# Routing weights of the first 128 tokens added into a DRAM table by GpSimd's indirect DMAs, those of the second 128 by one-hot products

## The chip, the cores and the metric

The kernel runs on one core of one Trainium2 chip. The metric is the device time of one execution in microseconds (us). The engines are TensorE (PE, with its weight loads PEld), VectorE (DVE), ScalarE (ACT), GpSimd (POOL) and SyncE (SP, which here issues DMAs only). ACT and POOL issue DMAs too.

## What is computed

Two transformer-like layers on 256 tokens of width 1024, in fp32. The change touches only the expert lookup ("peer") of the first layer. Of the reference, cut to that part:

```
qry = rms_norm((hb @ w_query).reshape(128, 8, 256), query_gain)      # hb: a block of 128 tokens
s1 = einsum("thd,nd->thn", qry[..., :128], sub_keys_1)                # (token, head, 128 keys)
s2 = einsum("thd,nd->thn", qry[..., 128:], sub_keys_2)
v1, i1 = top_k(s1, 16);  v2, i2 = top_k(s2, 16)
cand_s = v1[..., :, None] + v2[..., None, :]                          # 16 x 16 sums for each token and head
cand_i = i1[..., :, None] * 128 + i2[..., None, :]
top_s, pos = top_k(cand_s, 16)
experts = take_along_axis(cand_i, pos);  gates = softmax(top_s)
act = gelu(einsum("thkd,td->thk", expert_down[experts], hb))
out = einsum("thk,thkd->td", gates * act, expert_up[experts])
```

There are 128 x 128 = 16384 experts, and each token picks 8 x 16 = 128 of them.

## The kernel before, in words

The kernel gathers no expert rows. It computes gelu(hb @ expert_down) for all 16384 experts and all 256 tokens, multiplies it by a table G of gates that is zero where an expert was not picked, and multiplies the product by expert_up. Each fp32 factor of these large products is split into a high and a low float32r part: ACT writes the high part of a weight unit (128 x 512 words) in `split_hi` (L285), DVE the low part in `split_lo` (L290), and PE then does three products for each pair of tiles. There are four buffers of split units: ACT waits until PE is done with the unit four before (`unit_used`), DVE waits for ACT, PE waits for DVE. The weights themselves come by 1 MB DMAs from SP into a ring of four slots (`Stream`), four units each.

The stage in question is the Block at L1791. Its first part, "down", has 256 units (u = 0 to 255), 12 matmuls each (L1833). Every 8 units ACT applies Gelu to one group of 4 x 256 results (`gelu`, L1876) and stores it in `act_spill`. Everything else is woven between the units, in the order in which the code is written:

- DVE: `routing()` is a generator. After each unit's `split_lo`, DVE takes two or three of its steps (L2030): top 16 of 128 scores for 32 rows, sums, top 16 of 256 for 16 rows, then, for each tile of 128 tokens, the two key numbers of each pick by comparing with an iota, multiplying and reducing 128 x 2048 words. It must be finished at u = 154 (L2032). `step` (class `Steps`) attaches a semaphore to an instruction and makes DVE wait for it.
- ACT computes Exp of all picks at u = 155 (L1908), DVE divides by the sums, PE transposes the picks (L376) and DVE copies them out (L2043).
- From u = 161 to 247, six units of each eight carry a batch of gates of four tokens (`slots`, L1765). For a token DVE builds two one-hot matrices (L2007, L2010, `gated_onehots`), PE multiplies them (L1819), and the product is the token's 128 x 128 slab of gates; ACT copies four slabs from PSUM into G (L1897). There are 64 batches.

The second part, "up" (256 units, L300), loads the stored activations back in 32 pieces (`load_acts`, L1886), multiplies them by G (`weights`, L2017), splits them and multiplies by expert_up. POOL has nothing to do from the Block's start until `store_gate` and `load_gate` near its end. G lies on the words O_R and up; the routing's own scratch lies there as well, above its 83rd of 128 expert rows (`CLEAR`).

## Time and profile before

| | before |
|---|---|
| median of 3 runs | 1668.98 us (1668.96 to 1669.71) |
| span of the profiled execution, the only time that the page gives of it | 1673.4 us |
| PE busy | 1587.1 us, 95% |
| DVE busy | 1224.7 us, 73% |
| ACT busy | 906.1 us, 54% |
| POOL busy | 41.7 us, 2% |
| down products L1833 (PE) | first start 292.7, last 723.4 us |
| gate products L1819 (PE) | 530.6 to 709.0 us, 512 records, 67.9 us busy |
| gates written L1897 (ACT) | 64 copies, 37.0 us busy |
| one-hot matrices L2007, L2010 (DVE) | 512 instructions, 55.5 and 71.1 us busy |

Rows of the timeline give start, duration, engine, line, operation and names. Neighbouring instructions of one engine overlap by some 0.08 us, so what one costs on a full engine is read from the distance between starts. A row "x3" is three instructions in one stretch. "Idle before" counts only the engine's own idle time and names what ended it.

### The profile page before, as it was taken

The page shows a single profiled execution, that of the slowest core. Times are in us where ns is not written, and L with a number is a line of the kernel's source. Part 1 is how long each engine was busy: PE and PEld are TensorE (multiplying, and loading weights), DVE is VectorE, ACT ScalarE, POOL GpSimd, SP SyncE. Part 2 cuts the span into 40 slices and gives each one's busy share as a digit, 9 for nine tenths or more (in the row PEclk, how much of TensorE's full clock was granted, in tenths as well). Part 3 has the DMA queues.
Part 4 walks back from the last instruction along what each step waited for, and adds up shares of the span by engine and source line. Part 5 has one row for each costly group of instructions (what it writes and reads, how often), then busy time and mean ns, then how long its engine had stood idle before and what let it go on. Part 6 is the DMA issues. An engine that isn't in the chain of part 4 may idle for free. (4 is left out here: it accounts for less than half of the span.)

```text
span 1673.4 us, 26490 instructions
## 1 busy us (share of the span) xinstructions
PE 1587.1 (95%) x10351; PEld 1426.7 (85%) x10351; DVE 1224.7 (73%) x2475; ACT 906.1 (54%) x1518; POOL 41.7 (2%) x82
## 2 busy tenths in 40 slices
PE   5998888999999999999999999899999898989998
PEld 5877767999999999988888888797888677789997
DVE  5876765889997999867667777657886666654664
ACT  6775455554545555555555555546556646455453
POOL 0023000000000000000000000110000000000000
PEclk9999899999999999999999999999999899999999
DMA  9944343667766555567788767554443122445552
GB/s 327 364 161 128 102 159 125 213 217 235 229 205 213 158 158 151 165 229 248 237 293 289 250 234 245 202 177 151 151 150 128 63 89 101 151 151 177 181 197 101
DMA packets 111665, 313.85 MB, mean 188 GB/s; under 512 B 9441, under 2 KB 10041, under 8 KB 102073
## 3 DMA queue, kind: packets, MB, share of 16 engines
q1 hardware_dynamic: 100008, 276.95, 49.9%
q10 hardware_dynamic: 11040, 33.66, 5.9%
q8 instruction: 82, 1.34, 0.3%
q0 software_dynamic: 496, 1.59, 0.3%
q14 instruction: 39, 0.31, 0.1%
HBM read 293.28 MB, written 18.89 MB: 187 GB/s over the span
## 5 line engine op out<-in xcount | busy, mean ns | idle before, releaser
L300 PE MATMUL ps<-parts,parts 128*128 128x512 f32 (+1 forms) x4992 | 972.4, 357 | 20.1 <-DVE parts L290 18.1
L300 PEld LDWEIGHTS ps<-parts,parts 128*128 128x128 f32 x4992 | 824.3, 191 | 155.9 <-DVE parts L290 19.1
L285 ACT CAST parts<-lead 128x512 fp32r<-128x512 f32 x940 | 579.1, 620 | 619.9 <-PE ps L300 394.1
L290 DVE TENSOR_TENSOR parts<-lead,parts 128x512 fp32r<-128x512 f32 x940 | 641.1, 688 | 328.8 <-ACT parts L285 324.8
L1833 PE MATMUL ps<-parts,parts 128*128 128x256 f32 x3072 | 385.3, 285 | 4.5 <-DVE parts L290 4.5
L1833 PEld LDWEIGHTS ps<-parts,parts 128*128 128x128 f32 x3072 | 372.6, 192 | 5.6 <-DVE parts L290 5.6
L376 PE MATMUL ps<-lead,mem 128*128 128x128 f32 (+2 forms) x292 | 46.5, 323 | 41.0 <-ACT mem L520 23.2
L376 PEld LDWEIGHTS ps<-lead,mem 128*128 128x128 f32 (+2 forms) x292 | 40.9, 162 | 47.5 <-ACT mem L520 24.6
L2010 DVE TENSOR_SCALAR mem<-lead,mem 128x128 f32<-128x128 f32 x256 | 71.1, 341 | 0.0
L1819 PE MATMUL ps<-mem 128*128 128x128 f32 x512 | 67.9, 275 | 0.7 <-DVE mem L2010 0.7
L1819 PEld LDWEIGHTS ps<-mem 128*128 128x128 f32 x512 | 62.8, 192 | 1.2 <-issue 1.1
L2007 DVE TENSOR_SCALAR mem<-lead,mem 128x128 f32<-128x128 f32 x256 | 55.5, 280 | 0.0
L2017 DVE TENSOR_TENSOR mem<-mem 128x1024 f32<-128x1024 f32 x32 | 39.1, 1221 | 7.5 <-DMA mem<-act_spill 7.3
L2022 DVE TENSOR_TENSOR parts<-mem,parts 128x1024 fp32r<-128x1024 f32 x32 | 39.0, 1219 | 0.5 <-ACT parts L1893 0.5
L1897 ACT COPY mem<-ps 128x512 f32<-128x512 f32 x64 | 37.0, 579 | 0.0
L1893 ACT CAST parts<-mem 128x1024 fp32r<-128x1024 f32 x32 | 33.5, 1047 | 5.7 <-DVE mem L2017 5.7
L1876 ACT ACTIVATE mem<-ps 128x1024 f32<-128x1024 f32 x32 | 32.7, 1020 | 0.8 <-PE ps L1833 0.8
L2198 PEld LDWEIGHTS ps<-mem 128*128 128x128 f32 x256 | 29.8, 192 | 0.6
L2198 PE MATMUL ps<-mem 128*128 128x128 f32 x256 | 29.9, 275 | 0.0
L1348 PEld LDWEIGHTS ps<-mem 64*64 64x64 f32 x512 | 18.2, 151 | 6.3 <-POOL mem L1333 4.0
L1348 PE MATMUL ps<-mem 64*64 64x64 f32 x512 | 19.5, 238 | 4.3 <-POOL mem L1333 2.5
L479 POOL DMA_DIRECT2D gate_rows<-mem x1 | 0.6, 577 | 885.9 <-DVE mem L2066 885.9
(348 smaller groups left out, 994.3 us busy)
## 6 DMA issues: line engine op xcount, KB each, us to landing
lead<-in_peer_expert_down SPq DMA_DIRECT2D x64, 1024.0 KB, 5.5
lead<-in_peer_expert_up SPq DMA_DIRECT2D x64, 1024.0 KB, 5.8
lead<-in_w_in SPq DMA_DIRECT2D x50, 1024.0 KB, 5.2
lead<-in_w_ffn_in SPq DMA_DIRECT2D x22, 1024.0 KB, 5.2
act_spill<-mem ACTq DMA_DIRECT2D x32, 512.0 KB, 5.1
mem<-act_spill ACTq DMA_DIRECT2D x32, 512.0 KB, 3.6
mem<-in_w_ada SPq DMA_DIRECT2D x29, 512.0 KB, 6.9
lead<-in_w_ffn_out SPq DMA_DIRECT2D x11, 1024.0 KB, 4.9
```

Of the source, the lines that this page charges most:

```text
L285: act.copy(w_hi[g % BUFFERS], st.words(n, u * UNIT, UNIT)).then_inc(hi_ready, 1)
L290: dve.tensor_tensor(w_lo[g % BUFFERS], st.words(n, u * UNIT, UNIT), w_hi[g % BUFFERS].bitcast(F32), ALU.subtract).then_inc(lo_ready, 1)
L300: mm = pe.matmul(o, lhs[a], rhs[b], start=start and i == 0, stop=stop and i == 2, skip_group_check=True, **kw)
L376: last = pe.transpose(o, i, ident[0:i.shape[0], 0:i.shape[0]])
L1348: mm = pe.matmul(ps[rows, bank, u % 4 * HP:(u % 4 + 1) * HP], left[rows, :], right[rows, :], start=True, stop=True)
L1819: mm = pe.matmul(ps[:, 4 + b % 4, j * P:(j + 1) * P], one1[b % 2][:, j, :], one2[b % 2][:, j, :], start=True, stop=True)
L1833: mm = pe.matmul(ps[:, c % 2 * 2 + m // 2, m % 2 * S:(m % 2 + 1) * S], parts[a][:, ms], (x_hi, x_lo)[b][:, k, :], start=k == 0 and i == 0 ...
L2007: one = dve.tensor_scalar(one1[b % 2][:, j, :], iota, pick(0, b * GT + j), None, ALU.is_equal)
L2010: one = dve.tensor_scalar(one2[b % 2][:, j, :], iota, pick(1, b * GT + j), pick(2, b * GT + j), ALU.is_equal, ALU.mult)
L2017: dve.tensor_tensor(got[q % 2], got[q % 2], at(O_R + q * 1024, 1024), ALU.mult).then_inc(s_pr, 1)
L2022: dve.tensor_tensor(a_lo[q], got[q % 2], a_hi[q].bitcast(F32), ALU.subtract).then_inc(s_al, 1)
L2198: mm = pe.matmul(psf[:, 2048 + u * P:2048 + (u + 1) * P], k, q, start=True, stop=True)
```

## The change

Gates of the second 128 tokens are still made by one-hot products: 32 batches instead of 64, three of every eight units from u = 161 on, written into the right half of G. The left half of G now holds the activations of the first 128 tokens: `gelu` is two ACT instructions of 512 words instead of one of 1024, the first writing straight into G, the second to a buffer that is stored in `act_spill`, which is half as large.

Gates of the first 128 tokens go into a new DRAM table of 128 x 16384 words. Four Blocks earlier POOL zeroes a tile of 1024 words, and one Block later SP writes the 8.4 MB table from it with four DMAs, after its last `w_ada` load. In the down part the routing of the first 128 tokens is done in four pairs of heads, 19 units each (`pair_routing`), with one Exp on ACT for each pair; the routing of the others follows from u = 76 (`routing`). For each pair POOL then issues 2 x 16 indirect DMAs of 128 words with accumulation, one word from each partition; before each head it waits until all DMAs of the head before have landed. At u = 251 ACT waits until all 128 have landed. In the up part each of the 32 pieces comes by two DMAs of 256 KB, one from the table and one from `act_spill`.

The diff, cut to its core:

```diff
@@ SP and POOL, delta-rule stage
+                pool.memset(blank, 0.0).then_inc(s_blank, 1)
...
                 load_fills(sp, PE_SUMS[1] + FILLS, 3 * KT)
+                sp.wait_ge(s_blank, 1)
+                for i in range(4):
+                    sp.dma_start(gate_table[:, i * 4096:(i + 1) * 4096].rearrange("p (a b) -> p a b", b=1024),
+                                 blank.unsqueeze(1).to_broadcast([P, 4, 1024])).then_inc(s_cleared, 16)
@@ expert stage
-        NB4 = S // GT
+        NB4 = P // GT
         GATE0 = 20
+        PAIRS = NH // 2
+        GU = 19
-        slots = [8 * c + u for c in range(GATE0, 31) for u in (1, 2, 3, 5, 6, 7)][:NB4]
+        slots = [8 * c + u for c in range(GATE0, 31) for u in (1, 4, 6)][:NB4]
@@ GpSimd
+                for hd in range(NH):
+                    pool.wait_ge(s_pair, hd // 2 + 1)
+                    if hd:
+                        pool.wait_ge(s_put, 16 * TOP * hd)
+                    for j in range(TOP):
+                        c = hd * TOP + j
+                        pool.indirect_dma_start(
+                            out=cells, out_offset=bass.IndirectOffsetOnAxis(ap=picks[0][:, c:c + 1].bitcast(U32), axis=0),
+                            in_=picks[1][:, c:c + 1], in_offset=None, compute_op=ALU.add).then_inc(s_put, 16)
                 store_gate(pool)
@@ TensorE
-                            transposes(pe, [(psf[:, 2048 + (i * TT + tt) * P:2048 + (i * TT + tt + 1) * P],
-                                             pickT[:, i, tt * P:(tt + 1) * P])
-                                            for i in range(3) for tt in range(TT)]).then_inc(s_t, 1)
+                            transposes(pe, [(psf[:, 2048 + i * P:2048 + (i + 1) * P], pickT[:, i, :])
+                                            for i in range(3)]).then_inc(s_t, 1)
@@ ScalarE
-                    act.activation(staged, psf[:, c % 2 * 1024:(c % 2 + 1) * 1024], ACT.Gelu).then_inc(s_G, 1)
+                    act.activation(G[:, 4 * c:4 * c + 4, 0:P], tiles[:, :, 0:P], ACT.Gelu)
+                    act.activation(staged[c % 2].rearrange("p (m t) -> p m t", t=P), tiles[:, :, P:S], ACT.Gelu)\
+                        .then_inc(s_G, 1)
...
+                    for half, table in enumerate((gate_table, act_spill)):
+                        act.dma_start(got[q % 2][:, half * 512:(half + 1) * 512], table[:, q * 512:(q + 1) * 512])\
+                            .then_inc(s_rd[q % 2], 16)
...
+                    if u % GU == GU - 1 and u // GU < PAIRS:
+                        act.wait_ge(s_route, u // GU + 1)
+                        v = picks[1][:, pair_cols(u // GU)]
+                        act.activation(v, v, ACT.Exp).then_inc(s_e, 1)
...
                     if u == KT * DG - 5:
                         act.wait_ge(s_gm, NB4)
+                        act.wait_ge(s_put, 16 * TOP * NH)
+                        load_parts(0)
@@ VectorE
+                def pair_routing(r):
+                    rows, heads = range(4 * r, 4 * r + 4), range(2 * r, 2 * r + 2)
+                    yield from top16(score, best, best_at, rows)
+                    step(dve.tensor_copy(best_ix[:, rs, :], u32(best_at[:, rs, :])))
...
+                    yield from sums(heads, 4 * r)
+                    yield from top16(cand, picked, picked_at, heads)
...
+                    one = dve.tensor_tensor(pair_eq, wide(pair_of.rearrange("p r j -> p (r j)"), TOP),
+                                            iota[:, 0:TOP].unsqueeze(1).to_broadcast([P, 4 * TOP, TOP]), ALU.is_equal)
+                    for _ in range(3):
+                        yield
+                    step(one)
...
+                    one = dve.tensor_reduce(found.rearrange("p r j -> p (r j)"), pair_eq, AX, ALU.add)
+                    for _ in range(3):
+                        yield
+                    step(one)
...
...
+                    dve.tensor_copy(u32(picks[0][:, pair_cols(r)]), full_ix.rearrange("p h j -> p (h j)"))
+                    dve.tensor_tensor(picks[1][:, pair_cols(r)].rearrange("p (h j) -> p h j", j=TOP), pk,
+                                      pk[:, :, 0:1].to_broadcast([P, 2, TOP]), ALU.subtract).then_inc(s_route, 1)
+                def pair_gates(r):
+                    dve.wait_ge(s_e, r + 1)
...
-                    for _ in range(3 if u % 4 == 3 else 2):
-                        next(route, None)
+                    r, v = divmod(u, GU)
+                    if r < PAIRS:
+                        if v == 0:
+                            route = pair_routing(r)
+                        for _ in range(3 if v % 2 else 2):
+                            next(route, None)
+                        if v == GU - 2:
+                            for _ in route:
+                                pass
```

How this moves instructions, on the two engines where it matters. First DVE in the down part, where L290 (L291 after) is the low part of a unit. Before, at the end of the last top 16 and in the first search for key numbers:

```order
L290 TENSOR_TENSOR parts_52<-lead,parts_51 128x512
L1956 MAX_INDEX mem<-mem 128x8
L1977 TENSOR_SCALAR mem<-mem 128x128
L1978 TENSOR_SCALAR mem<-mem 128x128
L1979 CAST mem<-mem 128x256
L1983 TENSOR_TENSOR mem<-mem,lead 128x2048
L290 TENSOR_TENSOR parts_52<-lead,parts_51 128x512 x2
L1990 TENSOR_TENSOR mem<-mem 128x256 x2
```

After, the end of the first pair, units 12 to 19:

```order
L291 TENSOR_TENSOR parts_52<-lead,parts_51 128x512
L2028 TENSOR_SCALAR mem<-mem 128x2x16
L2029 TENSOR_SCALAR mem<-mem 128x2x16
L2032 CAST mem<-mem 128x64
L2035 TENSOR_TENSOR mem<-mem,lead 128x1024
L2041 TENSOR_TENSOR mem<-mem 128x1024
L2045 TENSOR_REDUCE mem<-mem 128x64
L2051 TENSOR_SCALAR mem<-mem 128x32
L2054 SCALAR_TENSOR_TENSOR mem<-mem 128x32
L2058 CAST mem<-mem 128x32
L2060 TENSOR_TENSOR mem<-mem 128x32
L1987 MAX mem<-mem 128x8 x2
```

The search, and the small instructions around it, now come after 12 units and once for each pair, and one more row of small ones after them. Second ACT at the same place. Before, units 12 and up:

```order
L285 CAST parts_51<-lead 128x512
L1880 DMA act_spill<-mem 128x1024
L285 CAST parts_51<-lead 128x512 x7
L1876 ACTIVATE mem<-ps 128x1024
```

After, units 13 to 20:

```order
L286 CAST parts_51<-lead 128x512 x6
L1951 ACT_TABLE_LOAD
L1951 ACTIVATE mem<-mem 128x32
L1914 ACT_TABLE_LOAD
L1914 ACTIVATE mem<-ps 128x4x128
L1915 ACTIVATE mem<-ps 128x512
```

The Exp of the first pair (L1951) stands between units 18 and 19, with a table load of its own, and the next Gelu loads its table again.

## Rows read from the trace of the kernel before

**Rows 1.** The page, part 1: busy time and share, instructions.
```profile
PE 1587.1 (95%) x10351; PEld 1426.7 (85%) x10351; DVE 1224.7 (73%) x2475; ACT 906.1 (54%) x1518; POOL 41.7 (2%) x82
```

**Rows 2.** Windows: length, busy and count of PE, PEld, DVE, ACT, POOL, clock, DMA.
```profile
400.00:460.00 60.00, 60.00 (x502) 60.00 (x502) 59.40 (x178) 29.98 (x47) 0.00 (x0) 1.00 0.72 234
...
575.00:600.00 25.00, 25.00 (x216) 25.00 (x216) 23.52 (x85) 13.63 (x23) 0.00 (x0) 1.00 0.47 134
```

**Rows 3.** Windows, PE alone, while DVE searches the key numbers.
```profile
460.00:480.00 20.00, 18.94 (x156) 1.00 0.66 216
480.00:500.00 20.00, 18.86 (x153) 1.00 0.64 211
```

**Rows 4.** Waits from 292 to 530 us: total us, times, longest.
```profile
ACT parts L285 <- PE ps L1833: 115.6, 138, 1.9
DVE parts L290 <- ACT parts L285: 23.1, 61, 2.5
PE ps L1833 <- DVE parts L290: 4.5, 5, 2.4
```

**Rows 5.** Timeline, DVE alone: distances between starts.
```profile
295.50 0.67 DVE L1940 MAX8 mem<-mem 128x8 f32<-128x128 f32 x3
296.09 0.67 DVE L290 TENSOR_TENSOR parts<-lead,parts 128x512 fp32r<-128x512 f32 x1
296.68 0.48 DVE L1940 MAX8 mem<-mem 128x8 f32<-128x128 f32 x2
...
453.19 0.08 DVE L1956 MATCH_VALUE_LOAD mem<-mem 128x8 f32 x1
...
453.60 0.07 DVE L1956 MATCH_VALUE_LOAD mem<-mem 128x8 f32 x1
...
455.11 0.23 DVE L1977 TENSOR_SCALAR mem<-mem 128x128 uint32<-128x128 uint32 x1
455.37 0.23 DVE L1978 TENSOR_SCALAR mem<-mem 128x128 uint32<-128x128 uint32 x1
...
717.78 1.22 DVE L2017 TENSOR_TENSOR mem<-mem 128x1024 f32<-128x1024 f32 x1
```

**Rows 6.** Lines by form, DVE, 292 to 530 us: busy, mean, idle before.
```profile
L1944 DVE FIND_INDEX8 mem<-mem 128x8 uint32<-128x128 f32 x32 | 8.7, 284 | 0.0
```

**Rows 7.** Timeline around the one Exp before, and the transposes.
```profile
516.64 1.28 ACT L1908 ACT_TABLE_LOAD   x1
...
518.89 1.29 DVE L290 TENSOR_TENSOR parts<-lead,parts 128x512 fp32r<-128x512 f32 x2 [2.47 <-ACT parts L285]
...
524.96 0.82 PE L376 MATMUL ps<-lead,mem 128*128 128x128 f32 x6
```

**Rows 8.** POOL's DMA issues: busy and mean ns, and idle before.
```profile
L706 POOL DMA_DIRECT2D mem<-rel_ext x2 | 1.8, 919 | 6.4 <-DMA rel_ext<-mem 6.4
L484 POOL DMA_DIRECT2D lead<-gate_rows x1 | 0.6, 579 | 3.0 <-DMA gate_rows<-mem 3.0
```

**Rows 9.** DMA issues of 1040 to 1060 us: KB, us to landing.
```profile
gate_rows<-mem POOLq DMA_DIRECT2D x1, 4.0 KB, 3.2
```

**Rows 10.** Timeline, DVE beside L706, which POOL runs from 49.89 us.
```profile
49.11 1.22 DVE L787 SCALAR_TENSOR_TENSOR lead<-lead 128x1024 f32<-128x1024 f32 x1
```

**Rows 11.** Timeline: SP around the place of the clearing, ACT's first query unit.
```profile
171.68 4.67 SPq L441 DMA_DIRECT2D mem<-in_w_ada  x3
198.81 15.98 SPq L94 DMA_DIRECT2D lead<-in_peer_w_query  x4
...
222.81 0.62 ACT L285 CAST parts<-lead 128x512 fp32r<-128x512 f32 x1 [0.32 <-PEq L1518]
```

**Rows 12.** DMA issues: stores to DRAM, KB each, us to landing.
```profile
x_spill<-mem SPq DMA_DIRECT2D x1, 1024.0 KB, 4.2
act_spill<-mem ACTq DMA_DIRECT2D x32, 512.0 KB, 5.1
```

**Rows 13.** Timeline, PE at the start of the up part.
```profile
734.52 5.76 PE L300 MATMUL ps<-parts,parts 128*128 128x512 f32 x17 [2.27 <-DVE parts L290]
```

More of the change, by code:

```diff
@@ L1242, in _ @@
                 pool.wait_ge(s_zero, 1)
+                pool.memset(blank, 0.0).then_inc(s_blank, 1)
+                pool.wait_ge(s_blank, 1)
                 pool.wait_ge(s_dexp, 2)
@@ L1958, in top16, with sums @@
                     step(one)
+                def sums(heads, row0):
+                    for n in heads:
+                        a, b = best[:, row0 + 2 * (n - heads[0]), :], best[:, row0 + 2 * (n - heads[0]) + 1, :]
+                        one = dve.tensor_tensor(cand[:, n, :].rearrange("p (a b) -> p a b", b=TOP), wide(a, TOP),
+                                                b.unsqueeze(1).to_broadcast([P, TOP, TOP]), ALU.add)
+                        yield
+                    step(one)
@@ new lines, in pair_gates @@
+                def pair_gates(r):
+                    dve.wait_ge(s_e, r + 1)
+                    v = picks[1][:, pair_cols(r)].rearrange("p (h j) -> p h j", j=TOP)
+                    total, inverse = tiny[:, 2 * r:2 * r + 2], tiny[:, 32 + 2 * r:34 + 2 * r]
+                    one = dve.tensor_reduce(total, v, AX, ALU.add)
+                    yield
+                    step(one)
+                    one = dve.reciprocal(inverse, total)
+                    yield
+                    step(one)
+                    dve.tensor_tensor(v, v, wide(inverse, TOP), ALU.mult).then_inc(s_pair, 1)
@@ L1960, in routing @@
                 def routing():
-                    yield from top16(score, best, best_at, range(TT * 2 * NH))
-                    step(dve.tensor_copy(best_ix, u32(best_at)))
+                    rs = slice(2 * NH, 4 * NH)
+                    yield from top16(score, best, best_at, range(2 * NH, 4 * NH))
+                    step(dve.tensor_copy(best_ix[:, rs, :], u32(best_at[:, rs, :])))
                     yield
-                    for tt in range(TT):
+                    yield from sums(range(NH, 2 * NH), 2 * NH)
@@ new lines, in routing @@
+                    yield from top16(cand, picked, picked_at, range(NH, 2 * NH))
+                    at_ = u32(at(O_V + 1792 + P, P))
+                    step(dve.tensor_scalar(u32(part_u[:, 0, :]), at_, 4, None, ALU.logical_shift_right))
+                    step(dve.tensor_scalar(u32(part_u[:, 1, :]), at_, 15, None, ALU.bitwise_and))
+                    step(dve.tensor_copy(part_of, u32(part_u)))
+                    yield
+                    eq = at(O_M, P, TOP)
+                    for half in range(2):
+                        step(dve.tensor_tensor(eq, wide(part_of[:, half, :], TOP),
+                                               iota[:, 0:TOP].unsqueeze(1).to_broadcast([P, P, TOP]), ALU.is_equal))
+                        for _ in range(5):
+                            yield
@@ L1966, in routing @@
                         for hd in range(NH):
-                            a = best[:, tt * 16 + 2 * hd, :]
-                            b = best[:, tt * 16 + 2 * hd + 1, :]
-                            one = dve.tensor_tensor(cand[:, tt * NH + hd, :].rearrange("p (a b) -> p a b", b=TOP), wide(a, TOP),
-                                                    b.unsqueeze(1).to_broadcast([P, TOP, TOP]), ALU.add)
+                            e3 = eq[:, hd * TOP:(hd + 1) * TOP, :]
+                            ix = best_ix[:, 2 * NH + 2 * hd + half, :]
@@ L2000, in routing @@
+                        step(one)
+                        step(dve.tensor_reduce(pickT[:, half, :], eq, AX, ALU.add))
+                        for _ in range(5):
+                            yield
+                    pk = picked[:, NH:2 * NH, :]
+                    step(dve.tensor_tensor(pickT[:, 2, :].rearrange("p (h j) -> p h j", j=TOP), pk,
+                                           pk[:, :, 0:1].to_broadcast([P, NH, TOP]), ALU.subtract))
                     dve.drain().then_inc(s_route, 1)
@@ L2029, in _ @@
                     split_lo(dve, n0 + u // UPC, g0 + u, u % UPC, 0)
-                    for _ in range(3 if u % 4 == 3 else 2):
-                        next(route, None)
+                    r, v = divmod(u, GU)
[7 more added lines that the diff above has]
+                                pass
+                    else:
+                        if u == GU * PAIRS:
+                            route = routing()
+                        for _ in range(3 if u % 4 == 3 else 2):
+                            next(route, None)
+                    if 1 <= r <= PAIRS:
+                        if v == 1:
+                            gate = pair_gates(r - 1)
+                        if 1 <= v <= 3:
+                            next(gate, None)
                     if u == KT * GATE0 - 6:
```

124 lines of the change are left out of this document (74 added, 50 removed).

## The prediction

> **What bounds the kernel now.** I read the page's busy times first, then the windows of the down part, then the waits there, then single rows. The page says PE 95% busy, POOL 2% [rows 1]; that names a suspect, no more. The windows say what PE's full stretches contain. Without gates 502 matmuls fit into 60 us [rows 2], so one takes 0.1195 us and a unit of 12 takes 1.434 us. With gates 216 records fit into 25 us; eight units and six batches are 96 + 48 = 144 records, 16.67 us. The waits agree: from 292 to 530 us ACT waited 115.6 us for PE to free a unit, PE only 4.5 us for DVE [rows 4]. So PE sets the pace of the down part, and what is taken off PE there is gained, as long as DVE keeps its place. That is the doubtful part: DVE is 59.4 of 60 us busy where the top 16 of 256 runs, and 23.5 of 25 us beside the gates [rows 2]. DVE loses its place once already: between 460 and 500 us PE did 309 matmuls, 36.9 us worth, in 40 [rows 3].
>
> **Gate products, the gain.** 24 gates cost 16.67 less 8 x 1.434 = 11.47, that is 5.2 us, 0.216 us each. 128 gates are removed: **-27.7 us**. Nothing else takes their time: ACT is half idle, and DVE has per eight units 12 fewer pairs of one-hot matrices. The picks need three transposes instead of six, and six took 0.82 us [rows 7]: **-0.4**. The search for key numbers with 128x2048 words is done for one tile, not for two; it lost 3.1 us of PE, so **-1.5**.
>
> **Pair routing, the cost.** Its instructions are those of the first tile moved to the first 76 units, with more small ones. The distances between starts give [rows 5, 6]: a split 0.59 us; a maximum over 128 words 0.20; a match load and a search over 256 words 0.41, over 128 about 0.27 (a mean of 0.284 less the overlap); a small instruction behind a step 0.26 for 128 words, I take 0.22 for 32 and 64; 128x1024 words 1.2. The row without a neighbour that I need is the maximum over 256: 0.33, between 0.20 and 0.41. A pair is then
>
> - units 0 to 8: 9 splits 5.3, four rows of 2 x 0.20 + 3 x 0.27 = 1.2 each (4.8), two sums 0.7, one cast 0.2, the gates of the pair before 0.6, step latencies 0.6: 12.2 us, against 9 x 1.434 = 12.9, so 0.7 to spare;
> - units 9 to 12: 4 splits 2.4, two rows of 2 x 0.33 + 3 x 0.41 = 1.9 each (3.8), steps 0.6: 6.8 against 5.7, late by 1.1;
> - units 13 to 17: 5 splits 3.0, three instructions of 1024 words with their steps 3.7, seven small 1.5: 8.2 against 7.2, late by 1.0;
> - unit 18: ACT waits for the end of the pair, loads a table (1.28) and does Exp before it makes the next high part. Before, the same wait left DVE idle for 2.47 us once [rows 7], with the Exp of 256 words; with 32 words, 2.1 from the end of the routing to unit 19, against 1.4: late by 0.7. After the first pair a Gelu with its table load follows at once (the order above), 1.6 more.
>
> What covers this is DVE's lead over PE. ACT writes a high part when PE is done with the unit four before; with 0.62 us for it, 0.69 for the low part and 0.1 for semaphores, 4.3 - 1.4 = 2.9 us are left. The first pair makes DVE 2.8 + 1.6 us late, so PE loses 1.5. Each later pair recovers 0.7 and then loses 2.8, of which 0.7 is covered: 2.1 x 3 = 6.3, less what the estimates of small instructions overstate. I take **+7**. The ends: 0, since each pair misses by only 10% of its 27.2 us; and 13, if every small instruction costs 0.26 and a table load after each Exp counts in full. If this cover is not there at all, it is the next paragraph's price. From unit 76 on the second tile needs 78 x 0.59 + about 56 = 102 us in 78 x 1.434 = 112: no loss.
>
> **Edits at nothing.** Two Gelus of 512 instead of one of 1024: some 0.2 us more each on ACT, which waits 115.6 us for PE in this stretch [rows 4]. POOL's zeroing of 1024 words stands where POOL waits for ACT anyway. The Exp of the pairs adds no PE work. `store_gate` stands behind the scatter on POOL, but it is wanted only near 1047 us. In the up part each piece needs a second DMA issue on ACT; ACT has slack, and only the first loads are exposed (PE lost 2.27 us there [rows 13]): **+0.5**.
>
> **The scatter.** The trace has no indirect and no accumulating DMA, so its cost T on POOL is bounded. POOL's plain issues are 0.58 and 0.92 us busy, the longer one for 1024 rows of 512 bytes [rows 8]; reading 128 indices and writing 128 descriptors should be near these, from 0.6 up. From above: if one waits for the landing of the one before, 3.2 us, what POOL's small store took [rows 9]. The deadline: the first pair's gates are ready near 292.7 + 22 x 1.434 + 2 = 326 us. ACT reaches unit 251 at 292.7 + 247 x 1.434 + 124 x 0.216 + 7 = 681 us. With 3 us for each of the eight landings, T may be (681 - 326 - 24) / 128 = 2.6 us before anything is late. I take T = 1.3, twice the short row, which ends at 517 us: hidden, **0**.
>
> A rule speaks against this. The trace first: while POOL issued L706 for 0.9 us from 49.89 us on, a DVE instruction with two inputs ran from 49.11 us in 1.22 us, the same as elsewhere [rows 10, 5], and POOL's issue was done in 0.92 us [rows 8]. The Trainium skill, SBUF — State Buffer, "SBUF: two separate sides" and the section behind it on a bandwidth pool, says that DVE and GpSimd share a port pair that one holds for a whole instruction, and that a GpSimd DMA of some 620 ns took some 3100 ns beside a DVE copy. By that page T would be up to 3.1 us and the scatter an estimated 65 us late; by the row it is hidden. DVE is nearly always busy here, so that rule is one reason for the fourth rival.
>
> **Clearing the table.** The four DMAs follow SP's last `w_ada` issue at 176.3 us; the next ones in SP's queue are the query weights from 198.8 us, first used at 222.8 us [rows 11]. 8.4 MB at the rate of the x store (1 MB in 4.2 us) take 34 us, to 210 us: the query weights still land before 222.8 us. At the rate of an act_spill store (0.5 MB in 5.1 us) they take 84 us [rows 12], to 260 us, and the query stage starts up to 37 us late. The second rate contains a landing latency for each 0.5 MB, which four queued DMAs do not pay one by one, so I take the first: **0**, bounds 0 and +37.
>
> **Sum**: -27.7 - 0.4 - 1.5 + 7 + 0.5 = -22.1 us. The span of the profiled execution is 1673.4 us, 4.4 above the median of 1668.98; the difference is the same for both kernels, so 1669.0 - 22.1 = **1647 us**.
>
> **Rivals.**
> 1. DVE's overload is absorbed and only the products count: 1669.0 - 29.1 = 1640 us. For it: the misses are 10% of a pair. Against: DVE was full for 60 us already.
> 2. POOL's descriptor work takes time from DVE: if each of the some 50 scatters within the overloaded units holds DVE for 0.25 us, 13 us more: 1660 us. Against it rows 10, which show one such place and no lengthening.
> 3. Clearing collides with the query weights, half of its bound: 1647 + 18 = 1665 us.
> 4. The scatter becomes the bound, the rival on the other side. At the last units of the down part ACT waits for the last landing, and PE stands for want of the next units. It decides from T = 2.6 us; from T = 2.6 + 22/128 = 2.8 us the kernel is slower than before. At T = 3.2, one at a time, it ends at 326 + 410 = 736 us, 55 us late: 1702 us. For it: accumulating word by word in DRAM is new here, and the indices and the ring are read and written beside a busy DVE. Against: the plain issues of 0.6 to 0.9 us, and that 16 may be in flight.
> 5. That the products are not what bounds PE in the gate stretch, and nothing is gained there: PE does 216 records in 25 us with no wait, so this has next to no chance.
>
> **How the numbers follow.** Forecast (1640 to 1656 on its own) 0.50, rival 1 0.12, rival 2 0.13, rival 3 0.08, rival 4 0.17. Rivals 1 to 3 are all faster. Leaving out rival 4, the range is 1638 to 1680: rival 1 below, rival 3 with a part of its bound above. A run tells some 0.2%, 3.3 us, from no change. Faster by more 0.80: the forecast and rivals 1 and 2, and most of rival 3; within 0.2% 0.03, where one of the costs just eats the gain; slower 0.17.
>
> **What would show it.** Right: L1819's counterpart has 256 records and the gate stretch is 27 us shorter; PE waits for DVE grow from 4.5 to about 10 us before unit 76, at the ends of the pairs; POOL's DMA rows have distances under 2 us and end before 600 us; no wait of ACT at unit 251; the first query split stays at 222.8 us. Wrong: POOL's rows at a distance of 2.6 us or more with ACT's wait for the scatter behind them (rival 4); DVE rows of 1.2 us growing longer beside them (rival 2); the query stage's first split late (rival 3); PE's waits for DVE no longer than before (rival 1).

## The result, and the profile after

| | before | after |
|---|---|---|
| median (5 runs each, same chip) | 1669.71 us (1668.96 to 1673.16) | 1663.24 us (1658.85 to 1666.32) |
| ratio, with its 95% interval | | 0.9946 (0.9930 to 0.9962) |
| span of the profiled execution | 1673.4 us | 1664.6 us |
| stage start to first down product | 292.7 us | 290.5 us |
| down products, first to last start | 292.7 to 723.4: 430.7 us | 290.5 to 706.3: 415.8 us |
| last down product to the first of L2198 (L2326 after), the next stage's | 439.8 us | 446.4 us |

The kernel became 0.5% faster, some 6 to 9 us, where 22 were forecast, and 1663 us lies in the range of 1638 to 1680. The down stage gained 14.9 us in the profiles, not 22, and the up part lost 6.6, which was not forecast. What lies before and behind them differs by 2 us between these two profiles, and by up to 6 us between those of all runs; it carries no argument.

The page of the changed kernel, part 1 and five rows of part 5, answers to [rows 1, 4, 8]. POOL's 128 scatters took 212.6 us of work that had no counterpart; PE's wait for DVE in the down products stayed at 4 us (2.4 of them, in both kernels, before the very first unit); but PE stood before the gate products, and DVE stood for the activations, which it had done for 7.3 us in the kernel before.

```profile
PE 1565.2 (94%) x10092; PEld 1399.4 (84%) x10092; DVE 1170.9 (70%) x2251; ACT 900.4 (54%) x1530; POOL 255.1 (15%) x212
...
L1871 PE MATMUL ps<-parts,parts 128*128 128x256 f32 x3072 | 377.8, 284 | 4.0 <-DVE parts L291 4.0
...
L1830 POOL DMA_INDIRECT gate_table<-mem x128 | 212.6, 1661 | 131.8 <-issue 74.5
...
L2128 DVE TENSOR_TENSOR mem<-mem 128x1024 f32<-128x1024 f32 x32 | 39.1, 1220 | 17.1 <-DMA mem<-act_spill 17.1
L1857 PE MATMUL ps<-mem 128*128 128x128 f32 x256 | 35.4, 281 | 10.5 <-issue 9.6
```

The windows of the changed kernel, with the columns of [rows 2]. Against [rows 2, 3]: PE is nearly as full as before up to 480 us, with DVE at 19.93 of 20 us; and in the gate stretch, where half the gate products are gone, PE has lost its fullness: 311 records in 40 us.

```profile
400.00:460.00 60.00, 60.00 (x503) 60.00 (x502) 53.41 (x191) 31.72 (x53) 43.03 (x26) 1.00 0.82 216
460.00:480.00 20.00, 20.00 (x169) 20.00 (x168) 19.93 (x67) 10.44 (x18) 11.52 (x8) 1.00 0.75 189
480.00:500.00 20.00, 19.34 (x161) 19.14 (x160) 19.72 (x34) 8.94 (x15) 14.01 (x9) 1.00 0.67 172
...
600.00:640.00 40.00, 37.57 (x311) 36.70 (x310) 26.20 (x77) 18.59 (x35) 25.45 (x16) 1.00 0.63 161
```

The stretch of the pairs from 300 us on, PE alone (length, busy and records, clock, DMA), before and after: PE did 10 matmuls fewer in the same 160 us, 1.2 us of its time.

```profile
300.00:460.00 160.00, 160.00 (x1336) 1.00 0.70 228
```

```profile
300.00:460.00 160.00, 159.46 (x1326) 1.00 0.77 208
```

The timeline of the changed kernel in the gate stretch, PE, ACT and DVE (start, duration, engine, line).

```profile
601.06 4.55 PE L1871 MATMUL ps<-parts,parts 128*128 128x256 f32 x36
...
602.78 0.62 ACT L286 CAST parts<-lead 128x512 fp32r<-128x512 f32 x1 [1.71 <-PE ps L1871]
...
603.43 0.69 DVE L291 TENSOR_TENSOR parts<-lead,parts 128x512 fp32r<-128x512 f32 x1 [1.56 <-ACT parts L286]
...
604.04 0.86 DVE L2116 TENSOR_SCALAR mem<-lead,mem 128x128 f32<-128x128 f32 x4
604.82 1.18 DVE L2119 TENSOR_SCALAR mem<-lead,mem 128x128 f32<-128x128 f32 x4
...
606.11 1.13 PE L1857 MATMUL ps<-mem 128*128 128x128 f32 x8 [0.49 <-issue]
606.99 4.55 PE L1871 MATMUL ps<-parts,parts 128*128 128x256 f32 x36
...
612.03 1.13 PE L1857 MATMUL ps<-mem 128*128 128x128 f32 x8 [0.49 <-issue]
```

DVE was idle for 1.56 us and then made the one-hot matrices too late. They stand in its program behind the low part of the unit two further on (`if u - 2 in slot_of`), that waits for ACT's high part, and ACT waits until PE frees a buffer (four units). ACT got its buffer at 602.78 us. PE could have taken the batch at 605.4 us, behind its three units (601.06 + 4.30), but the way through ACT, the low part and the eight one-hot instructions lasted until 606.1 us: 3.3 us where 2.6 were left. From 606.11 to 612.03 are 5.92 us for three units (4.30) and a batch (0.89): 0.73 us lost. "issue" names no releaser here; the end of DVE's 604.82 row beside PE's 606.11 does. Before, with six batches in eight units, one batch's own time on PE gave DVE the start for the next. With units 1, 4 and 6 of each eight, two of three batches have none in the two units ahead: 21 of 32, times 0.73 is 15.3 us; the page's 9.6 us of "issue", at 0.49 each, are 20 such places. That argument rests on this timeline; experiments 1 and 2 test it. Two timelines of the changed kernel follow: the Exp of the first pair, beside [rows 7], and PE at the start of the up part, beside [rows 13].

```profile
313.06 1.28 ACT L1951 ACT_TABLE_LOAD   x1
...
314.60 0.23 DVE L2051 TENSOR_SCALAR mem<-mem 128x32 f32<-128x32 f32 x1
314.87 0.19 DVE L2054 SCALAR_TENSOR_TENSOR mem<-mem 128x32 f32<-128x32 f32 x1
315.09 0.18 DVE L2058 CAST mem<-mem 128x32 uint32<-128x32 f32 x1
315.19 0.18 DVE L2060 TENSOR_TENSOR mem<-mem 128x32 f32<-128x32 f32 x1
315.29 0.68 DVE L291 TENSOR_TENSOR parts<-lead,parts 128x512 fp32r<-128x512 f32 x1
315.40 0.23 ACT L1951 ACTIVATE mem<-mem 128x32 f32<-128x32 f32 x1 [1.06 <-DVE mem L2060]
315.54 0.60 ACT L286 CAST parts<-lead 128x512 fp32r<-128x512 f32 x1
```

```profile
713.10 3.02 PE L301 MATMUL ps<-parts,parts 128*128 128x512 f32 x12 [1.06 <-DVE parts L291]
717.82 3.38 PE L301 MATMUL ps<-parts,parts 128*128 128x512 f32 x12 [1.70 <-DVE parts L291]
```

In the first, the table load runs before the wait for DVE is over, not behind it, and the small instructions start 0.10 to 0.27 us apart. In the second, PE stands for 1.06 and 1.70 us where it stood for 2.27 us before, so the start of the up part is not where its 6.6 us were lost.

### The profile page after: what moved, and what is told of

The parts are those of the page before. It is cut to its first block and busy times, and to the rows that moved or that the text cites. A ratio compares the mean times of both kernels' runs of the same rounds, so it can differ in the third digit from the quotient of the medians.

```text
span 1664.6 us, 25938 instructions
## 1 busy us (share of the span) xinstructions
PE 1565.2 (94%) x10092; PEld 1399.4 (84%) x10092; DVE 1170.9 (70%) x2251; ACT 900.4 (54%) x1530; POOL 255.1 (15%) x212
## 5 line engine op out<-in xcount | busy, mean ns | idle before, releaser
L291 DVE TENSOR_TENSOR parts<-lead,parts 128x512 fp32r<-128x512 f32 x940 | 638.3, 688 | 363.4 <-ACT parts L286 359.0
L1871 PE MATMUL ps<-parts,parts 128*128 128x256 f32 x3072 | 377.8, 284 | 4.0 <-DVE parts L291 4.0
L1830 POOL DMA_INDIRECT gate_table<-mem x128 | 212.6, 1661 | 131.8 <-issue 74.5
L377 PE MATMUL ps<-lead,mem 128*128 128x128 f32 (+3 forms) x289 | 45.6, 321 | 39.2 <-ACT mem L521 23.2
L377 PEld LDWEIGHTS ps<-lead,mem 128*128 128x128 f32 (+3 forms) x289 | 40.1, 161 | 45.6 <-ACT mem L521 24.7
L1857 PE MATMUL ps<-mem 128*128 128x128 f32 x256 | 35.4, 281 | 10.5 <-issue 9.6
L1857 PEld LDWEIGHTS ps<-mem 128*128 128x128 f32 x256 | 31.1, 191 | 14.3 <-issue 14.3
L1935 ACT CAST parts<-mem 128x1024 fp32r<-128x1024 f32 x32 | 33.5, 1047 | 14.9 <-DVE mem L2128 13.6
L2119 DVE TENSOR_SCALAR mem<-lead,mem 128x128 f32<-128x128 f32 x128 | 36.7, 365 | 0.0
L2326 PEld LDWEIGHTS ps<-mem 128*128 128x128 f32 x256 | 29.8, 192 | 0.6
L2326 PE MATMUL ps<-mem 128*128 128x128 f32 x256 | 29.9, 275 | 0.0
L2116 DVE TENSOR_SCALAR mem<-lead,mem 128x128 f32<-128x128 f32 x128 | 28.9, 290 | 0.0
L788 DVE SCALAR_TENSOR_TENSOR lead<-lead 128x1024 f32<-128x1024 f32 x16 | 18.9, 1218 | 2.1 <-DMA lead<-in_w_ada 2.1
## 6 DMA issues: line engine op xcount, KB each, us to landing
gate_table<-mem SPq DMA_DIRECT2D x4, 2048.0 KB, 16.6
```

The lines of the kernel that those rows point to most:

```text
L291: dve.tensor_tensor(w_lo[g % BUFFERS], st.words(n, u * UNIT, UNIT), w_hi[g % BUFFERS].bitcast(F32), ALU.subtract).then_inc(lo_ready, 1)
L377: last = pe.transpose(o, i, ident[0:i.shape[0], 0:i.shape[0]])
L1830: pool.indirect_dma_start(out=cells, out_offset=bass.IndirectOffsetOnAxis(ap=picks[0][:, c:c + 1].bitcast(U32), axis=0), in_=picks[1][:, c ...
L1857: mm = pe.matmul(ps[:, 4 + b % 4, j * P:(j + 1) * P], one1[b % 2][:, j, :], one2[b % 2][:, j, :], start=True, stop=True)
L1871: mm = pe.matmul(ps[:, c % 2 * 2 + m // 2, m % 2 * S:(m % 2 + 1) * S], parts[a][:, ms], (x_hi, x_lo)[b][:, k, :], start=k == 0 and i == 0 ...
L2119: one = dve.tensor_scalar(one2[b % 2][:, j, :], iota, pick(1, b * GT + j), pick(2, b * GT + j), ALU.is_equal, ALU.mult)
```

## The experiments

Each ratio is against the kernel before on the same chip, with its 95% interval. "Down" is the distance from the first to the last down product, "up" from there to the next stage's first product, in the profile.

**1 and 2. The one-hot matrices.** First, one unit earlier in DVE's program:

```diff
-                    if u - 2 in slot_of:
-                        gated_onehots(slot_of[u - 2])
+                    if u - 1 in slot_of:
+                        gated_onehots(slot_of[u - 1])
```

> The changed kernel, but DVE makes the one-hot matrices of a batch one unit earlier (behind the low part of unit s + 1, not s + 2, for the batch that PE takes after unit s). Theory A (late one-hots): in the changed kernel two of three batches follow three units without a batch, DVE gets to their one-hots only after PE's unit s - 2, and PE stands for 0.73 us at each of 21 batches (the period from one such batch to the next is 5.92 us, of which 4.30 are units and 0.89 gates). Then this takes 21 x 0.73 = 15 us off, 1663 to 1648, and the 9.6 us of 'issue' before the gate matmuls go. Theory B (a batch between units of another kind of matmul costs a fixed 0.4 to 0.5 us when it stands alone, wherever its operands are made): no change, within 2 us of 1663.

Second, the changed kernel with its batches as close as before:

```diff
-        slots = [8 * c + u for c in range(GATE0, 31) for u in (1, 4, 6)][:NB4]
+        slots = [8 * c + u for c in range(GATE0, 31) for u in (1, 2, 3, 5, 6, 7)][:NB4]
```

> The changed kernel with the slots of the kernel before (six batches in eight units) for its 32 batches, which are then over after 43 units instead of 86. Theory A (late one-hots): only a batch that follows two or more units without one is late, at most one or two of six; some 7 instead of 21 waits of 0.73 us: 10 us off, 1653. Theory B (fixed cost of each batch that stands alone): two of six batches stand alone instead of all, but in the kernel before all 64 batches cost 0.87 us each with the same slots, so 32 cost 28 us against some 43 now: also 10 to 15 us off. This run tells little between A and B; it tells whether the spacing of the slots is the cause at all: if not, 1663.

Measured: 1644.88 us, 0.9846 (0.9828 to 0.9865), down 400.2, up 444.3; and 1648.75 us, 0.9876 (0.9854 to 0.9899), down 402.0. The page's row of the gate products and the window 600 to 640 us, first both of the early kernel, then the window of the close one:

```profile
L1857 PE MATMUL ps<-mem 128*128 128x128 f32 x256 | 33.8, 275 | 0.0
```

```profile
600.00:640.00 40.00, 40.00 (x341) 40.00 (x340) 29.75 (x90) 21.16 (x38) 25.49 (x15) 1.00 0.62 160
```

```profile
600.00:640.00 40.00, 40.00 (x339) 40.00 (x338) 25.33 (x65) 21.15 (x38) 27.72 (x17) 1.00 0.68 171
```

PE's wait before the gate products is gone in the first (0.8 us are left of it in the second, which had been expected to keep some 7 late batches), and the down stage is 15.6 us shorter than in the changed kernel in the first, 13.8 in the second; the first is 30.5 us shorter than before. The late one-hot matrices cost the 15 us; either more time for them or another spacing gives it back.

**3 and 6. The kernel before with its loads cut.** Third, each piece by two DMAs of 256 KB; sixth, by one DMA of 512 KB whose rows are 2 KB instead of 4 KB, in loads and stores.

```diff
-                    act.dma_start(got[q % 2], act_spill[:, q * 1024:(q + 1) * 1024]).then_inc(s_rd[q % 2], 16)
+                    for half in range(2):
+                        act.dma_start(got[q % 2][:, half * 512:(half + 1) * 512],
+                                      act_spill[:, q * 1024 + half * 512:q * 1024 + (half + 1) * 512]).then_inc(s_rd[q % 2], 16)
```

> The kernel before, with each load of activations in the up part as two DMAs of 256 KB (2 KB a row) instead of one of 512 KB (4 KB a row), from the same table. Theory A (the form of the load): two DMAs of 2 KB rows beside the weight stream land later, as in the changed kernel, where DVE waited 17.1 us for loads instead of 7.3 and PE lost some 6 us of the up part: 4 to 8 us slower than before, 1674 to 1677. Theory B (something else in the changed kernel, as the other order of the up part's weights or the DRAM table's place): no change, 1669.7 within 2 us.

```diff
-                    act.dma_start(got[q % 2], act_spill[:, q * 1024:(q + 1) * 1024]).then_inc(s_rd[q % 2], 16)
+                    act.dma_start(got[q % 2].rearrange("p (h x) -> p h x", h=2),
+                                  act_spill.rearrange("p (h x) -> p h x", h=2)[:, :, q * 512:(q + 1) * 512]).then_inc(s_rd[q % 2], 16)
```

> The kernel before with one DMA of 512 KB a piece as it was, but from a table laid out so that each partition's 4 KB are two rows of 2 KB (the stores write such rows too). Theory A1 (row size): the shorter rows get less of the DMA engines beside the weight stream, whose rows are longer: 1675 to 1677, as e3_before_split_loads. Theory A2 (number of DMAs): one DMA lands once, so 1670 to 1671, no change; DVE's wait for loads stays near 7 us.

Measured: 1676.92 us, 1.0047 (1.0029 to 1.0065); and 1670.14 us, 0.9991 (0.9977 to 1.0004). The page's row of DVE's product, first with two DMAs, then with short rows; the kernel before had 7.5.

```profile
L2019 DVE TENSOR_TENSOR mem<-mem 128x1024 f32<-128x1024 f32 x32 | 39.1, 1221 | 26.0 <-DMA mem<-act_spill 26.0
```

```profile
L2019 DVE TENSOR_TENSOR mem<-mem 128x1024 f32<-128x1024 f32 x32 | 39.1, 1223 | 5.3 <-DMA mem<-act_spill 5.0
```

Two DMAs for a piece cost 0.47% (5 us between the medians, 8 by the ratio) without any other part of the change, 2 KB rows nothing that can be measured. The nine runs of the third spread from 1675.88 to 1685.79 us, and its profile is of one of 1685.07: there PE waited 14.2 us for DVE in the up part instead of 5.6, and behind some such waits PE's granted clock falls. PE alone, the window of a wait and the next one, in the changed kernel (where 45 records fill 10 us at the full clock):

```profile
880.00:890.00 10.00, 8.23 (x37) 1.00 0.72 256
890.00:900.00 10.00, 10.00 (x38) 0.83 0.70 231
```

In the up part of the third kernel's profile the granted clock stood at the lower of its two levels for 24 us, before and in the changed kernel for 14 us. So a late load can cost PE more than its wait, and a part of the third kernel's loss in this profile is clock, (24 - 14) / 2 = 5 us at most.

**4. The changed kernel without the scatter.** The indirect DMAs and ACT's wait for them are left out, so the gates of the first 128 tokens stay zero.

```diff
-                    for j in range(TOP):
-                        c = hd * TOP + j
-                        pool.indirect_dma_start(
...
+                pool.wait_ge(s_pair, NH // 2)
...
-                        act.wait_ge(s_put, 16 * TOP * NH)
```

> The changed kernel without the 128 indirect DMAs and without ACT's wait for them; the gates of the first 128 tokens stay zero, everything else is done. Theory A: the scatter is hidden and takes nothing from the other engines: 1663 within 2 us. Rival (DVE and POOL share something, or the small accumulating writes delay weights and activations): the one-hot instructions, mean 290 and 365 ns beside the scatter, go back to 280 and 341 ns, and 3 to 8 us go, part of the 21 waits of PE among them.

Measured: 1664.31 us, 0.9956 (0.9939 to 0.9974), down 415.6: the changed kernel's time. The scatter was hidden. The second one-hot instruction on DVE, from 530 to 690 us, first in the changed kernel, then without scatters:

```profile
L2119 DVE TENSOR_SCALAR mem<-lead,mem 128x128 f32<-128x128 f32 x124 | 35.6, 366 | 0.0
```

```profile
L2110 DVE TENSOR_SCALAR mem<-lead,mem 128x128 f32<-128x128 f32 x124 | 34.5, 346 | 0.0
```

It was 20 ns longer beside POOL's work, some 3 us over 128 of them. At the late batches DVE has no slack, so a part of it is time: from unit 161 to 255 the products took 1.2 us less without scatters.

**5 and 8. One load for both halves.** Both rest on experiment 1. Fifth, gates and activations side by side in each row of one table, so that a load has 4 KB rows, but the clearing has rows of 512 bytes. Eighth, one DRAM tensor with all gates of a row first and then all activations: the clearing and the stores keep their shapes.

```diff
-                    sp.dma_start(gate_table[:, i * 4096:(i + 1) * 4096].rearrange("p (a b) -> p a b", b=1024),
-                                 blank.unsqueeze(1).to_broadcast([P, 4, 1024])).then_inc(s_cleared, 16)
+                    sp.dma_start(gate_table[:, i * 8192:(i + 1) * 8192].rearrange("p (a b) -> p a b", b=S)[:, :, 0:P],
+                                 blank[:, 0:P].unsqueeze(1).to_broadcast([P, 32, P])).then_inc(s_cleared, 16)
...
+                    act.dma_start(got[q % 2], gate_table[:, q * 1024:(q + 1) * 1024]).then_inc(s_rd[q % 2], 16)
```

> e1_onehots_early, with both halves in one DRAM table: for each expert row 128 words of gates and beside them 128 words of activations, so that a piece is again one DMA of 512 KB with rows of 4 KB, and G and its products are laid out as in the kernel before. In exchange the clearing and the 32 stores write pieces of 512 bytes. Theory A (the form of the loads costs the up part): the 5 us that the split loads cost the kernel before come back: e1_onehots_early's ratio 0.985 goes to about 0.982, 1640. Rival (the 512-byte rows cost as much at the clearing or at the stores, where ACT waits for a store before the next Gelu): no change or slower than e1_onehots_early; then the first query unit or a Gelu comes late in the profile.

```diff
+        both = nc.dram_tensor("gates_and_acts", (P, P * S), F32, kind="Internal").ap().rearrange("p (h x) -> p h x", h=2)
+        gate_table, act_spill = both[:, 0, :], both[:, 1, :]
...
+                    act.dma_start(got[q % 2].rearrange("p (h x) -> p h x", h=2), both[:, :, q * 512:(q + 1) * 512])\
+                        .then_inc(s_rd[q % 2], 16)
```

> The changed kernel with the one-hot matrices one unit earlier, and the table of gates and the stored activations now lie in one DRAM tensor of 128 x 2 x 16384 words, first the gates and then the activations of each row, so that each of the 32 pieces comes by one DMA of 512 KB (rows of 2 KB), while the clearing and the stores keep their shapes (rows of 16 KB and 2 KB). Theory A, the number of load DMAs is what costs: DVE's waits for the activations in the up part fall from some 17 to 5 to 8 us, the up part loses some 5 us, and with the clearing as cheap as in the changed kernel (SP issues of 4.5 us at most, no wait of PE at the start of the down stage) the time is 1645 - 5 = 1640 us, ratio 0.981 to 0.982 of the kernel before. Theory B, the later landing comes from reading two separate regions of DRAM, or from the rows' addresses: the waits stay at 17 us and the time at 1645, ratio 0.984 to 0.985.

Measured: 1644.95 us, 0.9837 (0.9815 to 0.9858); and 1638.46 us (1637.91 to 1643.14), 0.9795 (0.9775 to 0.9814), down 401.2, up 439.7. In the fifth the loads' wait fell to 7.4 us and the up part to 438.4, but the clearing took it back: the first down product started at 294.9 us, in experiment 1 at 289.9. SP's issues of it there (ns: shortest, median, longest; first and last start), and then PE's wait behind them, before the stage's start (2.4 us in the changed kernel at that place):

```profile
L1331 SPq DMA_DIRECT2D gate_table<-mem x4: 433/6644/8436, 173.9 to 189.3; - x4
```

```profile
PE ps L376 <- PEq L1325: 8.4, 1, 8.4
```

The changed kernel's clearing, and then the row of the eighth kernel's loads:

```profile
L1332 SPq DMA_DIRECT2D gate_table<-mem x4: 434/772/4453, 175.0 to 177.1; - x4
```

```profile
L2127 DVE TENSOR_TENSOR mem<-mem 128x1024 f32<-128x1024 f32 x32 | 39.1, 1222 | 5.3 <-DMA mem<-gates_and_acts 4.9
```

**7. How near DVE is to its limit.** Experiment 1 with 17 units for a pair of heads instead of 19 (`GU = 17`).

> e1_onehots_early with 17 units for a pair of heads instead of 19, the rest of its steps all behind the 16th. In the changed kernel a pair takes DVE 27.1 us from its first to its last unit, and 19 units take PE 27.25: nothing is lost. Theory A (it just fits, and DVE is the limit as soon as it does not): with 24.4 us for a pair DVE is 2.7 us late each time; the lead of 2.9 covers the first, PE loses some 8 us, 1645 to 1653. Rival 1 (the sizes of the prediction, 29.3 us a pair): 16 us, 1661. Rival 2 (DVE has room that its busy time hides, so pair routing was never near a limit): no change, 1645.

Measured: 1658.22 us, 0.9906 (0.9877 to 0.9936), down 408.4. PE's waits for DVE in the down products grew to 9.8 us. The time lies above the 1645 to 1653 us that were expected; the 8 us that were expected of the down stage came. Windows, first of experiment 1, then with 17 units:

```profile
360.00:380.00 20.00, 20.00 (x168) 19.90 (x167) 19.30 (x59) 13.02 (x21) 14.22 (x10) 1.00 0.75 212
380.00:400.00 20.00, 20.00 (x169) 20.00 (x169) 19.29 (x55) 11.78 (x20) 10.37 (x7) 1.00 0.76 197
```

```profile
360.00:380.00 20.00, 17.66 (x143) 17.08 (x142) 17.70 (x55) 10.42 (x18) 14.03 (x9) 1.00 0.64 156
380.00:400.00 20.00, 18.18 (x149) 17.77 (x148) 19.42 (x57) 10.88 (x19) 13.28 (x8) 1.00 0.69 186
```

The mechanism of the forecast's +7 is real; it begins behind the 19 units that the change gives a pair, and with 17 the down stage is 8.2 us longer. Of these 1.4 fall in the first four units, where the granted clock was 0.83 in this profile (290 to 300 us) and 1.00 in experiment 1's, so 6.8 are left for the pairs. The rest of the 13 us between the two kernels is in the up part (450.4 us), where DVE's waits for loads were longer in this profile (25.9 us) and the granted clock was at its lower level for 17 us instead of 10; why the loads came later, this run does not tell.

**9. The fourth rival, forced.** Experiment 1 with a further scatter of the same size, into a table that nobody reads, behind every second one: 192.

```diff
+                        if j % 2:
+                            pool.indirect_dma_start(
+                                out=bass.AP(other_table.tensor, 0, [[1, P * P * P], [1, 1]]),
...
-                        act.wait_ge(s_put, 16 * TOP * NH)
+                        act.wait_ge(s_put, 24 * TOP * NH)
```

> The changed kernel with the one-hot matrices one unit earlier, and behind every second scatter DMA another of the same size, with accumulation into a second DRAM table that nobody reads: 192 instead of 128; ACT waits at unit 251 for all of them. It tests the prediction's fourth rival, the bound in waiting. Theory A, POOL works at 1.86 us for each DMA whatever else runs: the scatter ends 64 x 1.86 = 119 us later, at 634 + 119 = 753 us, where PE is out of units near 683 us. PE stands about 74 us before the last five units, the down stage ends near 765 instead of 690, and the time is 1645 + 74 = 1719 us (1705 to 1735), ratio 1.02 to 1.04; a wait of ACT of some 75 us just before its unit 251. Theory B, POOL's rate is set by the landing waits between heads and not by the issues: the end moves by less than 60 us and the time stays below 1660 us. Theory C, more scatters slow DVE or PE elsewhere: the matmuls between 292 and 600 us fall behind those of the kernel with 128.

Measured: 1742.03 us, 1.0435 (1.0393 to 1.0476). The waits from 600 to 790 us (total, times, longest):

```profile
ACT parts L287 <- DMA other_table<-mem: 94.8, 1, 94.8
...
PE ps L1877 <- DVE parts L292: 92.1, 1, 92.1
```

The place and the mechanism are the rival's; the wait is 95 us, not 74. My 1.86 us for each DMA was the distance between two undisturbed issues. POOL also paused in the changed kernel, for 2 to 5 us at a time, where the profile names nothing; with all pauses but those for landings one DMA costs (212.6 + 74.5) / 128 = 2.24 us. What the pauses are stays open. By that number 64 more end at 634 + 143 = 777 us (773 measured), 94 us behind 683.

**10 to 12. Earlier loads.** ACT issues the loads of a piece 6 units earlier, as soon as their buffer is free; in experiment 1, in experiment 8, and in the kernel before.

```diff
-                    if i % 8 == 7 and q + 2 < UG:
+                    if i % 8 == (1 if q else 7) and q + 2 < UG:
```

> The changed kernel with the one-hot matrices one unit earlier (1644.9 us, ratio 0.985), and from the fourth piece on ACT issues the two loads of a piece 6 units (some 8 us) earlier, right after the low part that frees their buffer. In the changed kernel DVE multiplies a piece by its gates some 4 us after ACT issued its loads (ACT issues at 766.56, DVE wants them at 781.5 minus a piece of 10.9 us, each shown by the trace), and they land after 2.8 to 3.1 us in the median, with some later. Theory A, the second DMA costs only because this lead of 4 us is short: DVE's waits for the loads fall from 17.6 us to the first pieces' 3 to 5, the up part from 444 to 439 us or less, and the time to 1638 to 1640 us, ratio 0.979 to 0.982, as with one load. Theory B, the number of DMAs costs by itself (ACT's or the queue's time): the waits move elsewhere and the time stays at 1644 to 1646.

> The kernel with one DRAM tensor and one load for each piece (1638.5 us, ratio 0.980) with that load 6 units earlier. Theory A, only the landing counts: its waits of DVE for the loads are 4.9 us, most of it at the first two pieces, whose loads are not moved, so at most 1 to 2 us are gained: 1637 to 1638, ratio 0.978 to 0.980. Theory B (of the run beside this one), where each DMA costs by itself: the same time as well, but then the kernel with two loads stays 6 us behind this one, while by theory A the two come to within 2 us of each other.

> The kernel before with its one load of 512 KB for each piece 6 units earlier, nothing else changed. Its waits of DVE for the loads are 7.3 us, of which 2.9 at the start. By theory A they fall to about 3 to 4 us and the time by 0 to 3 us, ratio 0.998 to 1.000. If the ratio falls further than 0.997, part of what the two kernels with early loads gain is not owed to the change, and has to be taken off the comparison.

Measured: 1639.85 us, 0.9800 (0.9780 to 0.9820), up 439.7; 1641.06 us, 0.9808 (0.9786 to 0.9830), up 439.7; 1670.36 us, 0.9990 (0.9977 to 1.0002). First, two loads in experiment 1, issue and use of a piece; then the same kernel with early loads, and its row on the page.

```profile
777.44 0.33 ACTq L1927 DMA_DIRECT2D mem<-gate_table  x1
777.80 0.86 ACTq L1927 DMA_DIRECT2D mem<-act_spill  x1
...
782.10 1.22 DVE L2128 TENSOR_TENSOR mem<-mem 128x1024 f32<-128x1024 f32 x1 [0.59 <-DMA mem<-act_spill]
```

```profile
774.73 0.45 ACTq L1927 DMA_DIRECT2D mem<-act_spill  x1
...
786.51 1.22 DVE L2128 TENSOR_TENSOR mem<-mem 128x1024 f32<-128x1024 f32 x1
```

```profile
L2128 DVE TENSOR_TENSOR mem<-mem 128x1024 f32<-128x1024 f32 x32 | 39.0, 1218 | 3.6 <-DMA mem<-act_spill 3.6
```

The loads had a lead of some 4 us (777.44 to 781.5, when DVE was ready), little more than the 2.8 and 3.1 us that they take to land in the median in the changed kernel. With 12 us of lead the second DMA costs nothing that can be measured: the medians with two loads and with one come within 1.2 us of each other, where they were 6.4 us apart (1644.88 and 1638.46). One load, or two early ones, do the same and don't add; all three bring the up part back to the 439.8 us of the kernel before. The kernel before gains nothing that can be measured from it, so the 2% of experiments 8, 10 and 11 are owed to the change and the two repairs. Of all kernels the eighth has the lowest time, and the tenth and eleventh can't be told from it.

## Why the prediction was wrong

The mechanism of the gain was right: its direction, and its size once the stage was mended (down -30.5 us in experiment 1 against -29.6 for products, transposes and search). The forecast missed because two costs were left out or priced at nothing, 15.6 and 6.6 us, while one that it had was too large, +7. Each part below is a distance between down products in the profiles, before and after. By its steps:

- **Gate products, -27.7, "Nothing else takes their time".** This is the step that failed. The count and the 0.216 us were right, but the removed products were also what gave DVE its lead over PE at the next batch. PE lost 0.73 us at 21 of 32 batches, 15.3 us by the timeline and 15.6 by experiment 1. With the transposes, units 160 to 255 took 14.3 us less than before instead of 28.1, and 29.9 less in experiment 1. The prediction looked at DVE's load (fewer one-hot matrices) and not at the path: PE frees a unit, ACT, DVE's low part, one-hot matrices, PE. Rival 5, that nothing is gained there, was nearly dismissed on the ground that PE had no wait before; half of it came true.
- **Search, -1.5.** Right: units 76 to 160 took 1.9 us less.
- **Pair routing, +7.** Mis-sized: +1.2, the time by which the first 76 units took longer (110.8 us instead of 109.5). ACT loads the Exp table while it waits for DVE, and small instructions of 32 words cost 0.10 to 0.27 us instead of 0.22 to 0.26 with steps. Which of the two made the difference was not tested. Experiment 7 shows that the limit stood close behind; that the cover held is rival 1.
- **Second load issue, +0.5.** Mis-sized: +6.6, and 5 to 8 alone in experiment 3. PE's own wait for DVE grew by 5.0 us of it (10.6 instead of 5.6); the rest is not split up, and lower clock behind the waits is one candidate. Its cost was taken as ACT's time for the issue; what mattered was a lead of 4 us before use (experiments 10 and 8).
- **Scatter, 0.** Right in its result, wrong in its number: T was 2.24 us, not 1.3 (which was called twice the short row of 0.58, and is more), and the bound 2.6: it came near, and the right result owes something to luck. It was done at 634 us with some 60 to spare; experiment 9 is rival 4. The landing waits between heads were near the 3 us assumed: 22.6 us for 6 of them, 3.8 each.
- **The port rule.** The trace has little of it: an indirect DMA took 1.56 us in the median, from 400 to 460 us beside a DVE busy for 53 of 60 us, and experiment 4 found DVE's one-hot instruction 20 ns longer beside it. By the figure in the Trainium skill, SBUF — State Buffer, "A bandwidth-pool intuition that's wrong (but worth ruling out)", which the page gives for a GpSimd DMA beside a DVE `tensor_copy`, it would have been up to 3.1 us for each and the scatter some 65 us late, an estimate. DVE runs mostly other instructions than that copy here; the measurement decides, and it was not late. Rival 2 is worth 1.2 us by experiment 4 (units 161 to 255), not 13.
- **Clearing, 0.** Right: it took 6.6 us of SP's queue, and PE's wait before the stage was 2.4 us. Experiment 5 shows what the other end was made of: the issues, not the bytes.

The sum with the measured terms: -29.9 + 15.6 - 1.9 + 1.2 + 6.6 = -8.4 us, where the spans give -8.8 and the medians -6.5.

## What to carry to other kernels

Work that is removed from the bounding engine may have been the cover for a latency: before counting it as gain, follow the loop from "buffer free" through the helpers back to that engine and compare its length with what is left between two uses. Here a load's cost was not its issue but its landing against its lead; when one DMA becomes two, look how long before use they are issued, and move them as far ahead as the buffer allows. A queue that waits behind nothing visible still pauses: take an average over a long stretch, not the distance of two neighbours.

## What the hardware showed unasked

- An indirect accumulating DMA of 128 words keeps POOL for 1.56 us in the median, with 0.30 to the next; 2.24 us with its pauses.
- SP's issue of 2 MB to DRAM took 0.4 to 4.5 us each in pieces of 4 KB (772 ns in the median), and up to 8.4 us in pieces of 512 bytes (6.6 us in the median); the landing was 16.6 us in the median for both.
- ACT's table load ran ahead of the wait that its own activation stood in (313.06 us, the activation at 315.40).
- In experiment 9 PE stood for 92 us; its granted clock was 0.50 from 690 to 780 us and 0.95 from 780 to 790, after PE had started again at 777 us.
